# A diagonal matrix of gate over sum in the attention's turn, in place of a VectorE scaling and a transpose

## The reference, cut to what matters

```
s = einsum("bqghd,bkgd->bghqk", qblk, k)            # one branch
s = s - slopes * distance                           # and -inf where the key is later than the query
p = softmax(s, axis=-1)
o_branch = einsum("bghqk,bkgd->bqghd", p, v)
o = gate0 * o_cmp + gate1 * o_slc + gate2 * o_win   # gates: sigmoid, one per token and head
```

## Time and profile before

| what | value |
|---|---|
| median of 3 runs | 2300.84 us (2299.89 to 2302.17) |
| the profiled execution | 2299.34 us, of which 2297.5 us span from first to last instruction |
| mean granted TensorE clock | 0.968 |
| TensorE busy | 2160.2 us, 94% |
| VectorE / ScalarE / GpSimd busy | 1142.9 / 742.3 / 770.4 us |
| attention stage | first score product at 762.0 us, last value products at 929.9 us |

### The profile page before, as it was taken

How to read it: one execution, slowest core, us unless ns; L and a number is a source line. 1 busy time by engine, 2 the same in 40 slices (tenths; PEclk the granted TensorE clock), 3 DMA queues, 4 the chain that set the end, 5 groups by cost and what they waited for, 6 DMA issues and landing times.

```text
span 2297.5 us, 25830 instructions
## 1 busy us (share of the span) xinstructions
PE 2160.2 (94%) x9956; PEld 1705.1 (74%) x9956; DVE 1142.9 (50%) x1760; ACT 742.3 (32%) x1101; POOL 770.4 (34%) x198
## 2 busy tenths in 40 slices
PE   7999999999978788999999989999889998999999
PEld 6888877888867344788778867766568876888887
DVE  5546886233152688568742353556784745110111
ACT  4124211123222576332112243444234433221221
POOL 4444434434421210244334333221212223444433
PEclk9999999999988799999999989999989999999999
DMA  4223334222251000233332222111111112223222
GB/s 159 94 107 146 129 145 158 82 89 98 107 171 55 1 1 1 74 141 129 135 144 92 86 104 71 59 55 37 55 37 56 55 55 74 101 86 106 92 88 94
DMA packets 34202, 205.02 MB, mean 89 GB/s; under 512 B 4160, under 2 KB 5312, under 8 KB 14784
## 3 DMA queue, kind: packets, MB, share of 16 engines
q1 hardware_dynamic: 31968, 196.84, 24.4%
q10 hardware_dynamic: 2144, 6.95, 1.0%
HBM read 199.58 MB, written 2.10 MB: 88 GB/s over the span
## 4 chain that ended last, share of the span: by engine, by line
PE 62%; issue 21%; DVE 7%; POOL 6%; ACT 4%; ACTq 0%; DMA 0%; SPq 0%; POOLq 0%; DVEq 0%
PE PS L501 14%; PE PS L502 14%; PE PS L503 14%; POOL WL L441 6%; PE PS L797 2%; PE PS L799 2%; PE PS L798 2%; PE PS L711 1%; PE PS L699 1%; PE PS L686 1%; DVE XB L1908 1%; ACT PB L1255 1%; ACT PT L1264 1%; PE PS L845 1%; PE PS L877 1%
## 5 line engine op out<-in xcount | busy, mean ns | idle before, releaser
L441 POOL TENSOR_TENSOR WL<-WR,WH 128x2048 fp32r<-128x2048 f32 (+2 forms) x173 | 738.8, 4271 | 1365.0 <-ACT WH L1068 1365.0
L501 PE MATMUL PS<-Hh,WH 128*128 128x512 f32 x1632 | 646.6, 396 | 21.6 <-DVE Hl L1556 9.9
L502 PE MATMUL PS<-Hl,WH 128*128 128x512 f32 x1632 | 640.9, 393 | 0.0
L503 PE MATMUL PS<-Hh,WL 128*128 128x512 f32 x1632 | 640.0, 392 | 0.0
L1068 ACT ACTIVATE WH<-WR 128x2048 fp32r<-128x2048 f32 (+2 forms) x173 | 305.4, 1765 | 787.9 <-PE PS L503 689.1
L501 PEld LDWEIGHTS PS<-Hh,WH 128*128 128x128 f32 x1632 | 310.2, 190 | 91.8 <-issue 21.9
L502 PEld LDWEIGHTS PS<-Hl,WH 128*128 128x128 f32 x1632 | 310.0, 190 | 66.0 <-issue 2.2
L503 PEld LDWEIGHTS PS<-Hh,WL 128*128 128x128 f32 x1632 | 309.9, 190 | 65.3
L501 PE MATMUL PS<-Gh,WH 128*128 128x512 f32 x592 | 233.0, 394 | 16.2 <-POOL WL L441 16.2
L502 PE MATMUL PS<-Gl,WH 128*128 128x512 f32 x592 | 232.2, 392 | 0.0
L503 PE MATMUL PS<-Gh,WL 128*128 128x512 f32 x592 | 232.1, 392 | 0.0
(11 more groups left out here) (273 smaller groups left out, 2369.8 us busy)
## 6 DMA issues: line engine op xcount, KB each, us to landing
WR<-wA SPq DMA_DIRECT2D x125, 1024.0 KB, 4.8
AW<-wada SPq DMA_DIRECT2D x24, 1024.0 KB, 4.9
WR<-wB SPq DMA_DIRECT2D x24, 768.0 KB, 5.4
WR<-wC SPq DMA_DIRECT2D x24, 640.0 KB, 3.9
X<-x_in SPq DMA_DIRECT2D x8, 256.0 KB, 6.1
W1K<-w1k ACTq DMA_DIRECT2D x1, 2048.0 KB, 10.3
W1V<-w1v ACTq DMA_DIRECT2D x1, 2048.0 KB, 15.8
out<-X SPq DMA_DIRECT2D x8, 256.0 KB, 4.6
```

The costliest lines, as they stand in the source:

```text
L441: nc.gpsimd.tensor_tensor(WL[:, s, 0:n], WR[:, s, 0:n], WH[:, s, 0:n].bitcast(F32), ALU.subtract).then_inc(lo_s, 1)
L501: nc.tensor.matmul(PS[:, b, :], wh[:, c, cols], pe_h, start=c == 0, stop=False)
L502: nc.tensor.matmul(PS[:, b, :], wh[:, c, cols], pe_l, start=False, stop=False)
L503: last = nc.tensor.matmul(PS[:, b, :], wl[:, c, cols], pe_h, start=False, stop=c == seg.chunks - 1)
```

## The change

The probabilities stay unscaled in `PB`. VectorE multiplies the 128x128 identity by the same two per-row factors (reciprocal of the sum, gate) into a 128x128 tile `DIAG`, one for each of the 10 rows of the ring. TensorE then multiplies each block of `PB` with that diagonal matrix, as an ordinary float32 product, where it transposed the block before: the result is the turned and scaled block. Semaphores, order and everything else stay.

```diff
+        DIAG = [at(f"DIAG{k}", 52 + k / 2 if k < 8 else 65 + k / 2, [P, P]) for k in range(NPB)]
...
                         for kb in range(qb + 1):
-                            mm = nc.tensor.transpose(PS[:, (7, 3)[m % 2], kb * P:kb * P + P],
-                                                     PB[:, m % NPB, kb * P:kb * P + P], ident[:, :])
+                            mm = nc.tensor.matmul(PS[:, (7, 3)[m % 2], kb * P:kb * P + P],
+                                                  PB[:, m % NPB, kb * P:kb * P + P], DIAG[m % NPB][:, :],
+                                                  start=True, stop=True)
                         mm.then_inc(p_t, 1)
...
-                    w = P * qb + P
...
-                        nc.vector.tensor_scalar(PB[:, k % NPB, 0:w], PB[:, k % NPB, 0:w], RMX[:, k:k + 1],
+                        nc.vector.tensor_scalar(DIAG[k % NPB][:, :], ident[:, :], RMX[:, k:k + 1],
                                                 GT[:, qb, gate:gate + 1], ALU.mult, ALU.mult).then_inc(s_n, 1)
```

## The result

The changed kernel takes 2314.46 us in the median of 5 runs (2311.79 to 2320.28), the kernel before 2300.84 (5 runs, 2299.64 to 2302.61). The ratio is 1.0061, 95% interval 1.0045 to 1.0076: slower by 13.6 us, where 17.2 was forecast and 2318.0 predicted.

The account below looks back on a forecast made before the run. Bound: an order of waits, each cycle 3.46 us set by VectorE and ScalarE, 6.55 us by TensorE. 8 x 1.17 + 6 x 0.71 + 1.6 + 1.9 = 17.2 us more; predicted median 2318.0, range 2312 to 2328.

Parts of the forecast that it names:

- the 3.46 us stretch: From step-3 turn to second step-0 block, set by VectorE and ScalarE; claimed to stay 3.46 us.
- nine blocks of a cycle: Step 3's eight blocks and one of step 0: their nine extra records fall into TensorE's idle time, costing nothing.
- The idle time of 0.6 us: TensorE's waits before the second step-0 block in a regular cycle, claimed to shrink from 1.28 us to about 0.6.
- The price of a record: On TensorE every turned block costs one more record, 0.106 us at the high clock.
- The tail: End of the attention stage: 18 extra records, all on the path to the last value products, 1.9 us.
- The head: Before the first full cycle: extra records of steps 5 and 6, 1.5 us, plus 0.1 for the first step 0.
- the reserve that I had named: A busier TensorE keeping the high clock in 772 to 776 us would win up to 1.4 us back.
- Nothing absorbed: Rival: no step-3 record falls into idle time, all eight count in each full cycle; 11.9 us more, 2330; 9 in 100.
- More absorbed: Rival: all 26 us of TensorE's idle time in the window is filled, 8 us remain, 2309; 5 in 100.
- Faster by the scaling: Rival: VectorE's scaling, 12.8 us shorter, frees the turn earlier and longer products hide in idle time; 2288; 3 in 100.
- No difference: Rival: the change does not do what it says, one record for a product; 1 in 100.
- Four records' worth: Rival: a plain float32 block takes four times a transpose, about 77 us more, 2378; 2 in 100.

Follow-up runs that it names:

- the kernel with width 512 alone: Kernel before, with the product with DIAG only for tiles of width 512 (128 of 320 blocks), the others scaled and transposed as before: 2300.25 us, ratio 1.0006.
- the one with the three other widths: Kernel before, with the product with DIAG only for widths 128, 256 and 384 (192 blocks), width 512 scaled and transposed as before: 2314.10 us, ratio 1.0068.
- TensorE's half alone: Kernel before, rows scaled at full width as before, but turned by an ordinary product with the identity: 2316.43 us, ratio 1.0078.
- the kernel before with the copy first: Kernel before, with ScalarE's copy of the turned tile ahead of the exponential in each half step: 2286.22 us, ratio 0.9941.
- the two halves: Kernel before with only the diagonal tile written, rows transposed unscaled: 2299.29 us; or with only full-width scaling and a product with the identity: 2316.43 us.
- the three float32r kernels: Changed kernel with probabilities and diagonal tile in float32r: 2310.04 us; also with copy ahead of exponential: 2291.43 us; also with out_pair cut in two: 2288.53 us.

## Why the prediction was right

**The mechanism** held at each point that could be tested: the 3.46 us stretch stayed (3.47); nine blocks of a cycle fell into its waits (eight in the kernel with width 512 alone, and the ninth by the one with the three other widths, whose step 0 takes 0.16 us more and not 0.32); the cycles became one length; the scaling was worth nothing. What was off in the cycles is nearly all of one kind: cycles of 11.4 for 11.2 us, and the turns of steps 1 and 2 longer by 0.50 and 0.73 for 0.42 and 0.64. The median's own range, 14 to 19 us more, was missed by the first set of runs (13.6) and hit by the second (18.0); the wide range, 2312 to 2328, holds both.

**Two measures mixed.** The idle time of 0.6 us that I forecast was counted from the last start of the first step-0 block, while the 1.28 us that it was to shrink from are recorded waits, which begin at the modelled end of a product. In the first measure some 0.48 us are left, in the second 0.20. VectorE's saving of 12.8 us has the same fault: it sets 128 times a mean length (45.8) against a busy time in which overlaps count once (58.6). The sum of lengths before is 128 x 0.500 = 64.0, after it 128 x 0.368 = 47.1; both measures give 16.9 us less. Neither slip reached the sum: it adds up only the records behind the second step-0 block's start, and it costs the scaling at nothing.

**The price of a record** is the term that was mis-sized. I took 0.106 us from eight products of the second block, where sixteen records take 1.70 us to the next line. Here sixteen take 1.98 by the same measure. The turns of 4, 6 and 8 transposes took 0.59, 0.80 and 1.02 us to the next line, those of 8, 12 and 16 records 1.09, 1.53 and 1.98. That is 0.50, 0.73 and 0.96 for 4, 6 and 8 more, some 0.12 each, not 0.106; a single block of step 0 took 0.16 more. Of the 0.12, 0.11 is the spacing in a group and the rest a longer pause after it. A cycle thus grew by 0.16 + 0.50 + 0.73 = 1.39 where I had 1.17, and one with `out_pair` by 0.94 where I had 0.71: 8 x 1.39 + 6 x 0.94 = 16.8, the 16.78 measured, against 13.7.

**Head and tail.** The tail cost 2.14 (1.9 forecast). The head cost -0.76 in place of +1.6. Its blocks do take longer, but the granted clock is another. Before, it was 0.78 and 0.50 in the windows that begin 10 and 12 us after the stage's first score. In the changed kernel the windows that begin 9 and 13 us after it are these:

```profile
766.00:770.00 4.00, 3.00 (x21) 1.96 (x18) 3.31 (x19) 3.40 (x14) 0.00 (x0) 1.00 0.00 0
770.00:774.00 4.00, 4.00 (x31) 3.00 (x30) 3.09 (x13) 3.25 (x9) 0.52 (x1) 1.00 0.00 0
```

This is the reserve that I had named, up to 1.4 us back. The Trainium skill's rule of that place, that transposes do not count as activity in the way products do ("TensorE: Matmul & The Clock Gate", Part 4), would fit these two profiles, and the second profile of the changed kernel has the same head of 18.66 us. But two kernels speak against it. The one with TensorE's half alone has as many products and a clock of 0.62 from 11 to 15 us after its first score, and the kernel before with the copy first turns by transposes only and has 1.00 from 10 us after its first score to the first full cycle; cycles with transposes hold 1.00. So the cause is left open. The two errors of 3.1 and -2.4 nearly cancel, and the stage's 18.16 came close to 17.2 for a reason that was half luck.

**From the stage to the median.** The medians differ by 13.6 and 18.0 us in two sets of runs, and the stage by 18.16 us in each profile. The executions of one kernel scatter over 8 us and more, most of it in the untouched parts where two profiles could be compared, so the prediction of 2318.0 for a median of 2314.5 is as near as this measurement goes.

**The rivals.** Nothing absorbed: refuted by the width-512 kernel. More absorbed: refuted by the stage, 18.16 us longer where 8 would be left. Faster by the scaling: refuted by the two halves. No difference: refuted by the 640 records and the interval. Four records' worth: a block costs some 0.12 us over a transpose's 0.107, about twice. By the rule of the Trainium skill ("TensorE: Matmul & The Clock Gate", Terms) it would be four times; the measurement decides for two.

## What to carry to other kernels

A float32 transpose turned into a float32 product doubles TensorE's records. It is free just where TensorE waits for another engine anyway, so count the blocks step by step against the waits of that step, and not the sum against the sum of idle time. Taking work from an engine that sits beside the path wins nothing until the path is mended; here that was the order of two operations on ScalarE, 0.6%, after which VectorE's load began to count. Cutting the output work in two took a further 1.9 us from the full cycles. Where executions scatter by more than the effect, compare the stage in the profiles, by head, cycles and tail: in two profiles of one kernel it repeated to 0.01 us, but between kernels the head moved by 1.2 and 1.9 us where the clock in it differed.

## What the runs showed of the hardware

- The product of two float32 128x128 tiles leaves two weight loads and two products in the trace, a transpose or a float32r product one of each (640 and 320 records for the same 320 blocks).
- The spacing of such records is not the same everywhere: sixteen take 1.70 us to the next line in the second block, 0.106 each, and 1.98 us in this stage, where each further one adds 0.11.
- The granted clock stayed at its lower level in full cycles of the three float32r kernels while TensorE was recorded busy throughout (782 to 794 us of the one shown); the transposing kernels, with as many records and waits, kept the higher level there. With plain products it fell as well, in the tail of the kernel with the three other widths (0.55 from 935 to 938 us). Why is open.
- Two profiled executions of one kernel differed by 8.7 us in when the stage began, and by no more than 0.01 us in the stage.
